# Experts in blocks of 32 rows on four column tiles, with smaller edits in the combination and the windowed attention

## The chip, the core and the metric

The kernel runs on one core of a Trainium2 chip. One launch computes everything. The metric is the time of one execution on the device, in microseconds (us). The engines named here are TensorE (PE; its weight loads are shown apart, as PEld), VectorE (DVE), ScalarE (ACT), GpSimd (POOL), and SyncE (SP), which issues most transfers.

## The reference, cut to what matters

The reference is a layer of two blocks on 1024 tokens of 1024 features, all in fp32. The first block mixes tokens by two gated scans and then runs a mixture of 32 experts; the second has a gated linear scan, a windowed attention, an RWKV scan and a feed-forward net. The change touches the mixture, the sum that follows it, and the windowed attention:

```
g_idx = argmax(g_logits)                      # one of 4 groups of 8 experts
top_v, top_i = top_k(e_in_group, 2)           # two experts of the group, for each token
weights = g_w * softmax(top_v)
gate, up = split(xb @ e_w_in[e], 2)           # 1024 -> 2 x 512
y = (silu(gate) * up) @ e_w_out[e]            # 512 -> 1024
out[token] += y * weight                      # two assignments of each token
...
o = sum over (window, dilation) in ((128,1),(512,4),(2048,16)) of softmax-weighted banded causal attention
```

There are 2048 assignments of a token to an expert. The routing formula, evaluated on the reference's own inputs, gives the experts between 2 and 447 tokens; the largest have 447, 282, 127, 122, 115, 94, 88 and 68. An expert's weights are 12 chunks of 128 rows and 1024 columns, 512 KB each: eight for the first product and four for the second.

## The kernel before, in words

The kernel is a chain of stages, each of which ends in a barrier of all engines. Within a stage every engine has its own list of instructions, and semaphores order them.

**Routing (`stage_route`).** It picks the experts, and places each assignment in a slot of a block. A block has `BR` = 64 slots and belongs to one expert; every expert has at least one block. DVE builds the tables `low` and `high` (L2098 to L2103), PE turns them into slot numbers (L1973), and DVE into row numbers for the gathers and scatters. The experts' order is computed here too: `seat` spreads those with many blocks among those with one, the two experts of number 0 and 1 come first.

**Experts (`stage_experts`).** Each of the blocks is computed as follows. POOL gathers its rows of the tokens from DRAM (L2227): partition p < 64 holds the first half of a row's features, partition 64 + p the second half, so that a gather has 128 descriptors of 2 KB. PE transposes the rows (`turn`, L2278), ACT copies them to `xt`. `up` (L2287) multiplies eight chunks of weights. The tokens are the stationary operand, only 64 columns wide, so PE's array is used as two column tiles: `lanes(j)` is the half of the columns, and of PSUM's partitions, on which the product with half j of the weights' columns runs. ACT applies silu and copies, POOL multiplies the two (L2236), PE transposes the result (`turn_h`, L2294), ACT copies it, and `down` (L2304) multiplies four chunks, again on two tiles. ACT copies the result to `y` (L2337), and POOL scatters it to the rows of `moe_y` (L2231).

The loop is pipelined in software. PE's order is `up(i+1)`, `turn(i+2)`, `down(i)`, `turn_h(i+1)`. POOL's order in iteration i is: multiply for block i+1; wait until every scatter issued so far has landed (`s_st`, L2250 and L2251), which frees `y`; wait for `turn(i+2)`, which frees `xr`; gather block i+3; wait for ACT's copy of block i; scatter block i. There is one buffer `xr` for gathered rows and one `y` for results.

The weights come by SP's queue. `raw` has two slots for each chunk, and `w`, from which PE reads, has one. DVE copies a chunk of the next expert from `raw` to `w` (L2210) as soon as the last block of the present one has used it. ACT copies the four chunks of the second product for every block anew (L2344). SP requests a chunk once DVE, or ACT at an expert's last block, has emptied its slot. So while an expert is computed the transfers can be two experts ahead and no further.

**Combination (`stage_combine`).** For each of the eight tiles of 128 tokens, SP loads the two results (three buffers of each), ACT weights the one (`weighted`, L2405), DVE adds the other (`summed`, L2447), PE transposes (L2500), and DVE adds into the residual (`added`, L2453). For each quarter of 256 tokens ACT squares (L2411), PE forms two sums of squares (`means`, L2509 and L2511), ACT takes roots, and DVE scales.

**Windowed attention (`stage_window`, after the gated scan).** SP requests queries and keys, the mask and the values in three transfers (L2851 to L2853). PE's first scores (L2869) wait for the whole of the first.

Of the kernel before, what the change touches and what calls it, by code (L numbers as in the profile page):

```python
# [42 lines left out]
BR = 64  # L43
# [1821 lines left out]
def stage_route(K):  # L1865
# [8 lines left out]
    with K.stage() as st:  # L1874
# [19 lines left out]
        far, wrap, yf, side = sb("far", [P, NS]), sb("wrap", [P, NS]), sb("slot", [P, NS]), sb("side", [P, 1])  # L1894
        pt = [K.ps(f"route_turn{i}", [P, 2, BANK], st) for i in range(2)]
# [16 lines left out]
        with nc.Block() as block:  # L1912
# [14 lines left out]
            def _(pool):  # L1927
                pool.memset(K.exp_rows[:], 0.0).then_inc(s_zero, 1)
                for s in s_st:
# [3 lines left out]
                pool.indirect_dma_start(K.exp_rows[:], None, xrows.rearrange("t (a d) -> (t a) d", a=2), bass.IndirectOffsetOnAxis(ap=K.moe_xi[:, 0:1], axis=0),  # L1933
                                        bounds_check=2 * T - 1, oob_is_err=False).then_inc(K.s_rows, 16)

            @block.tensor
            def _(pe):
# [32 lines left out]
                for u in range(NU):  # L1970
                    if u in (0, NU // 2):
                        pe.wait_ge(s_hot, 2 if u == 0 else 4)
                    mm = pe.matmul(pv, low[:, u, :], high[:, u, :], start=u == 0, stop=u == NU - 1)  # L1973
# [5 lines left out]
            def _(act):  # L1979
# [3 lines left out]
                for i in range(NT):  # L1983
# [4 lines left out]
                    if i == 0:  # L1988
                        act.wait_ge(s_step, 6)
# [5 lines left out]
            def _(dve):  # L1995
# [48 lines left out]
                step(dve.tensor_reduce(side[:], K.c("ident")[:, BR:P], AX.X, ALU.add))  # L2044
                dve.wait_ge(s_lt, 1)
# [71 lines left out]
                step(dve.tensor_scalar(far[:], wrap[:], 2.0, side[:], ALU.mult, ALU.add))  # L2117
                step(dve.tensor_copy(K.moe_xi[:], far[:]))
                dve.sem_inc(s_xi, 1)
                step(dve.tensor_scalar(yf[:], yf[:], 2.0, side[:], ALU.mult, ALU.add))  # L2120
# [23 lines left out]
def stage_experts(K):  # L2144
# [4 lines left out]
    HALF = D // 2  # L2149
    xrows = K.scratch["moe_x"].rearrange("t (a d) -> (t a) d", a=2)  # L2150
    yb = K.dram("moe_y", [2 * T, D]).rearrange("t (a d) -> (t a) d", a=2)
    KE, FH = DE // P, DE // 2
    UP, DOWN = range(KT), range(KT, NCHUNK)
    with K.stage() as st:
# [5 lines left out]
        xr, xt = K.exp_rows, sb("x", [P, KT // 2, P])  # L2160
        h, hu, ht, y = sb("h", [P, FH]), sb("h_up", [P, FH]), sb("h_turned", [P, KE // 2, P]), sb("y", [P, HALF])
        cx, cy = (K.sb(f"exp_{n}", [P, 1], I32, stack=st, fill=False) for n in ("x_at", "y_at"))
        pt, pu, ph, py = (K.ps(f"exp_{n}", [P, *shape], st) for n, shape in (
            ("turn", [KT // 2, P]), ("up", [2, FH]), ("turn_h", [KE // 2, P]), ("down", [BANK])))
# [12 lines left out]
        with nc.Block() as block:  # L2177
# [47 lines left out]
            def _(pool):  # L2225
                def gather(at):
                    pool.indirect_dma_start(xr[:], None, xrows, bass.IndirectOffsetOnAxis(ap=at, axis=0),  # L2227
                                            bounds_check=2 * T - 1, oob_is_err=False).then_inc(s_x, 16)

                def scatter(at):  # L2230
                    pool.indirect_dma_start(yb, bass.IndirectOffsetOnAxis(ap=at, axis=0), y[:], None,  # L2231
                                            bounds_check=4 * T - 1, oob_is_err=False).then_inc(s_st, 16)
# [2192 lines left out]
```

## Time and profile before

| | us |
|---|---|
| median of 3 runs (lowest to highest) | 3363.76 (3363.58 to 3369.75) |
| the profiled execution's own time | 3360.97 |
| its span, first to last instruction | 3359.2 |
| PE busy (share of the span) | 2964.2 (88%) |
| DVE busy | 1747.2 (52%) |
| ACT busy | 1263.9 (38%) |
| POOL busy | 302.4 (9%) |
| blocks of experts computed | 48 |

The span is divided into 40 slices of 84 us in the page. Busy shares are averages over stages with different limits, and PE's is high nearly everywhere. Each fp32 matmul of the program appears as two records, so a chunk of `up` on two tiles has four. A record's duration includes the time in which the last results leave the array, and records overlap: the pace is read from starts, not from durations.

### The profile page before, as it was taken

The page shows a single profiled execution, that of the slowest core. Times are in us where ns is not written, and L with a number is a line of the kernel's source. Part 1 is how long each engine was busy: PE and PEld are TensorE (multiplying, and loading weights), DVE is VectorE, ACT ScalarE, POOL GpSimd, SP SyncE. Part 2 cuts the span into 40 slices and gives each one's busy share as a digit, 9 for nine tenths or more (in the row PEclk, how much of TensorE's full clock was granted, in tenths as well). Part 3 has the DMA queues.
Part 4 walks back from the last instruction along what each step waited for, and adds up shares of the span by engine and source line. Part 5 has one row for each costly group of instructions (what it writes and reads, how often), then busy time and mean ns, then how long its engine had stood idle before and what let it go on. Part 6 is the DMA issues. An engine that isn't in the chain of part 4 may idle for free. (4 is left out here: it accounts for less than half of the span.)

```text
span 3359.2 us, 46984 instructions
## 1 busy us (share of the span) xinstructions
PE 2964.2 (88%) x17182; PEld 2107.5 (63%) x17183; DVE 1747.2 (52%) x2670; ACT 1263.9 (38%) x2003; POOL 302.4 (9%) x447
## 2 busy tenths in 40 slices
PE   7999789879699999967999598577979999799988
PEld 5788667756333333326888596266758888687766
DVE  6221664652543032427644684765468777634554
ACT  5220223341344545435433433411234454433423
POOL 2000002510022222310000000000000000000000
PEclk9999889889799999988999798789989999999999
DMA  6331663834599598962433211101122222153432
GB/s 216 102 108 57 181 208 132 219 96 168 208 399 408 229 409 346 384 266 73 128 104 91 69 48 51 66 3 59 57 75 90 80 87 83 62 217 134 170 102 86
DMA packets 342397, 509.82 MB, mean 152 GB/s; under 512 B 46525, under 2 KB 239492, under 8 KB 339024
## 3 DMA queue, kind: packets, MB, share of 16 engines
q1 hardware_dynamic: 308128, 436.81, 37.6%
q0 software_dynamic: 16336, 44.15, 3.5%
q10 hardware_dynamic: 17760, 26.48, 2.3%
q8 instruction: 117, 1.92, 0.2%
q14 instruction: 56, 0.46, 0.0%
HBM read 431.42 MB, written 85.10 MB: 154 GB/s over the span
## 5 line engine op out<-in xcount | busy, mean ns | idle before, releaser
L2287 PE MATMUL exp_up_psum<-exp_w,exp_x 128*64 128x512 f32 x1536 | 342.6, 599 | 5.1 <-issue 4.4
L2287 PEld LDWEIGHTS exp_up_psum<-exp_w,exp_x 128*64 128x64 f32 x1536 | 106.8, 137 | 207.3 <-issue 206.2
L2210 DVE COPY exp_w<-hN 128x1024 f32<-128x1024 f32 x128 | 89.1, 696 | 259.6 <-PE exp_up_psum L2287 237.8
L2344 ACT ACTIVATE exp_w<-exp_w_raw_down 128x1024 f32 x188 | 185.4, 1056 | 39.2 <-DMA exp_w_raw_down<-in_expert_w_out 39.0
L2304 PE MATMUL exp_down_psum<-exp_w,exp_h_turned 128*64 128x512 f32 x768 | 177.5, 600 | 8.2 <-ACT exp_w L2344 8.1
L421 PE MATMUL down_ps_psum<-down_ah,down_wh 128*128 128x512 f32 x352 | 141.3, 401 | 24.1 <-DVE down_al L4168 24.0
L2210 DVE COPY exp_w<-exp_w_raw_up 128x1024 f32<-128x1024 f32 x128 | 90.7, 713 | 122.4 <-PE exp_up_psum L2287 104.2
L421 PE MATMUL in_ps_psum<-hN_hi,in_wh 128*128 128x512 f32 x336 | 134.3, 400 | 5.6 <-DVE hN_lo L809 5.5
L422 PE MATMUL down_ps_psum<-down_al,down_wh 128*128 128x512 f32 x352 | 137.8, 391 | 0.0
L423 PE MATMUL down_ps_psum<-down_ah,down_wl 128*128 128x512 f32 x352 | 137.6, 391 | 0.0
L422 PE MATMUL in_ps_psum<-hN_lo,in_wh 128*128 128x512 f32 x336 | 132.1, 393 | 0.0
L423 PE MATMUL in_ps_psum<-hN_hi,in_wl 128*128 128x512 f32 x336 | 132.0, 393 | 0.0
L4166 DVE TENSOR_TENSOR down_wl<-down_w,down_wh 128x512 fp32r<-128x512 f32 (+1 forms) x66 | 57.4, 870 | 141.9 <-ACT down_wh L4137 141.8
L3998 DVE TENSOR_TENSOR up_wl<-up_w,up_wh 128x512 fp32r<-128x512 f32 x133 | 91.7, 690 | 74.9 <-ACT up_wh L3894 74.8
L421 PE MATMUL wout_ps_psum<-mixF_hi,wout_wh 128*128 128x512 f32 x256 | 105.6, 412 | 14.2 <-DVE mixF_lo L1784 12.9
L3650 DVE TENSOR_TENSOR in_wl<-in_w,in_wh 128x512 fp32r<-128x512 f32 x91 | 62.6, 690 | 105.0 <-ACT in_wh L3574 105.0
L2304 PEld LDWEIGHTS exp_down_psum<-exp_w,exp_h_turned 128*64 128x64 f32 x768 | 49.9, 136 | 101.8 <-issue 90.0
L3894 ACT ACTIVATE up_wh<-up_w 128x512 fp32r<-128x512 f32 x133 | 83.3, 627 | 72.4 <-PE up_z_psum L3860 32.6
L413 DVE CAST in_wh<-in_w 128x1024 fp32r<-128x1024 f32 x21 | 14.6, 693 | 182.5 <-PE in_ps_psum L423 182.5
L3860 PE MATMUL up_x_psum<-up_hi_T,up_wh 128*128 128x512 f32 x264 | 103.2, 391 | 2.0 <-DVE up_wl L3998 1.3
L4137 ACT ACTIVATE down_wh<-down_w 128x512 fp32r<-128x512 f32 (+1 forms) x66 | 51.0, 773 | 140.3 <-PE down_ps_psum L423 128.5
L3860 PE MATMUL up_x_psum<-up_hi_T,up_wl 128*128 128x512 f32 x264 | 102.7, 389 | 0.0
(829 smaller groups left out, 7438.7 us busy)
## 6 DMA issues: line engine op xcount, KB each, us to landing
exp_w_raw_up<-in_expert_w_in SPq DMA_DIRECT2D x128, 512.0 KB, 15.7
exp_w_raw_down<-in_expert_w_out SPq DMA_DIRECT2D x128, 512.0 KB, 15.5
hN<-in_expert_w_in SPq DMA_DIRECT2D x128, 512.0 KB, 15.5
in_w<-in_w_in SPq DMA_DIRECT2D x50, 512.0 KB, 4.0
up_w<-in_ffn_up SPq DMA_DIRECT2D x88, 256.0 KB, 3.4
down_a<-ffn_act SPq DMA_DIRECT2D x66, 256.0 KB, 3.3
down_w<-in_ffn_down SPq DMA_DIRECT2D x22, 512.0 KB, 3.4
down_w<-in_ffn_down SPq DMA_DIRECT2D x44, 256.0 KB, 2.6
```

The costliest lines, as they stand in the source:

```text
L421: pe.matmul(out, r(w[0]), r(x[0]), start=start, stop=False)
L422: pe.matmul(out, r(w[0]), r(x[1]), start=False, stop=False)
L423: return pe.matmul(out, r(w[1]), r(x[0]), start=False, stop=stop)
L2210: dve.tensor_copy(w[:, c, :], raw[u][c]).then_inc(s_have[c], 1)
L2287: mm = pe.matmul(pu[lanes(j), :, :], xt[:, c % (KT // 2), lanes(c // (KT // 2))], f[:, :, j * FH:(j + 1) * FH], start=c == 0, stop=c == KT ...
L2304: mm = pe.matmul(py[lanes(j), :], ht[:, k % (KE // 2), lanes(k // (KE // 2))], w[:, c, j * HALF:(j + 1) * HALF], start=k == 0, stop=k == K ...
L2344: act.activation(w[:, KT + k, :], K.exp_down[:, bass.ds(r + k, 1), :].rearrange("p o n -> p (o n)"), ACT.Copy).then_inc(s_down[k], 1)
L3650: dve.tensor_tensor(wl[i % R][:].bitcast(F32R), stationary[op](n), wh[i % R][:], ALU.subtract).then_inc(s_al, 1)
L3860: mm = pe.matmul(out, r32(w[r][:, k, :]), r32(v[o][:, k, :]), start=opens and k == 0 and x == 0, stop=k == 3 and x == 2, skip_group_check= ...
L3894: act.activation(wh[i % R][:].bitcast(F32R), stationary[op](n), ACT.Copy).then_inc(s_ah, 1)
L3998: dve.tensor_tensor(wl[i % R][:].bitcast(F32R), stationary[op](n), wh[i % R][:], ALU.subtract).then_inc(s_al, 1)
L4166: dve.tensor_tensor(wl[s % R][:, 0:n].bitcast(F32R), wt[s % R][:, 0:n], wh[s % R][:, 0:n], ALU.subtract).then_inc(s_wl, 1)
```

## The change

`BR` becomes 32 and the array is used as four column tiles of 32. A row of features is cut in four pieces of 256: a gather and a scatter still have 128 descriptors, now of 1 KB, and `up` and `down` have twice as many matmuls, each of half the columns. Products, copies and buffers of a block halve (`KX` = 2 transposes in `turn`, one in `turn_h`). The routing has room for 96 blocks in place of 64, so its tables are 98 wide in place of 66. POOL's and SP's loops, the number of buffers `xr`, `y`, `raw` and `w`, ACT's copies of the second product's weights for every block, and the formula of the experts' order stay as they are.

In the combination there are four buffers in place of three, and ACT's order changes. In the attention the three requests become seven, the first three of them small, and the waits are put where the pieces are used.

```diff
-BR = 64
+BR = 32
+NPART = P // BR
 NBLK = 2 * T // BR + NE
...
+                for a in range(2, NPART):
+                    step(dve.tensor_reduce(later[:], K.c("ident")[:, a * BR:P], AX.X, ALU.add))
+                    step(dve.tensor_tensor(side[:], side[:], later[:], ALU.add))
...
-                    for a in range(2):
+                    for a in range(NPART):
                         dve.tensor_tensor(low[:, u, a * BR:(a + 1) * BR], iota[:, 0:BR].unsqueeze(1).to_broadcast([P, NU // 2, BR]),
...
-    KE, FH = DE // P, DE // 2
+    KE, FH = DE // P, DE // NPART
+    KX, KH = KT // NPART, KE // NPART
...
-                    for k in range(KT // 2):
+                    for k in range(KX):
                         mm = pe.transpose(pt[:, k, :], xr[:, k * P:(k + 1) * P], K.c("ident"))
...
-                        for j in U:
-                            mm = pe.matmul(pu[lanes(j), :, :], xt[:, c % (KT // 2), lanes(c // (KT // 2))], f[:, :, j * FH:(j + 1) * FH],
+                        for j in range(NPART):
+                            mm = pe.matmul(pu[lanes(j), :, :], xt[:, c % KX, lanes(c // KX)], f[:, :, j * FH:(j + 1) * FH],
                                            start=c == 0, stop=c == KT - 1)
...
-                        for j in U:
-                            mm = pe.matmul(py[lanes(j), :], ht[:, k % (KE // 2), lanes(k // (KE // 2))], w[:, c, j * HALF:(j + 1) * HALF],
+                        for j in range(NPART):
+                            mm = pe.matmul(py[lanes(j), :], ht[:, k % KH, lanes(k // KH)], w[:, c, j * PIECE:(j + 1) * PIECE],
                                            start=k == 0, stop=k == KE - 1)
...
-    NT, NB, NQ = T // P, 3, 4
+    NT, NB, NQ = T // P, 4, 4
...
-                for i in range(3):
+                for i in range(NB):
                     weighted(i)
                 for q in range(NQ):
                     squares(q)
-                    for i in (2 * q + 3, 2 * q + 4):
+                    for i in (2 * q + 4, 2 * q + 5):
...
-                for i in range(3):
+                for i in range(NB):
                     turn(i)
                 for q in range(NQ):
-                    if 2 * q + 3 < NT:
-                        turn(2 * q + 3)
                     means(q)
-                    if 2 * q + 4 < NT:
-                        turn(2 * q + 4)
+                    for i in (2 * q + 4, 2 * q + 5):
+                        if i < NT:
+                            turn(i)
...
-                sp.dma_start(qkF[:], qk.rearrange("(a p) t -> p a t", p=P)).then_inc(s_qk, 16)
-                sp.dma_start(wide[:], K.wide_dram[:, 0:T]).then_inc(s_mask, 16)
-                sp.dma_start(v[:], vT[:, 512:768].rearrange("(c t) v -> t c v", t=P)).then_inc(s_v, 16)
+                sp.dma_start(qkF[:, 0::2, 0:EARLY], rows[0][:, :, 0:EARLY]).then_inc(s_qk[0], 16)
+                sp.dma_start(wide[:, T - EARLY:T], mask[:, T - EARLY:T]).then_inc(s_mask[0], 16)
+                sp.dma_start(v[:, 0:2, :], values[:, 0:2, :]).then_inc(s_v[0], 16)
+                sp.dma_start(qkF[:, 0::2, EARLY:T], rows[0][:, :, EARLY:T]).then_inc(s_qk[1], 16)
...
+                    if u in (0, 2, NT):
+                        pe.wait_ge(s_qk[(0, 2, NT).index(u)], 16)
```

PE in the body of the experts' loop, before (the text after a name is the shape of one matmul's output, xN their number; ISA is an instruction that only steers):

```order
L2287 MATMUL exp_up_psum<-exp_w,exp_x 64x512 x16
L2276 ISA
L2278 MATMUL exp_turn_psum<-const,exp_rows 128x128 x4
L2304 MATMUL exp_down_psum<-exp_w,exp_h_turned 64x512 x8
L2294 MATMUL exp_turn_h_psum<-const,exp_h 128x128 x2
```

And PE at the same place in the changed kernel:

```order
L2293 MATMUL exp_up_psum<-exp_w,exp_x 32x256 x32
L2282 ISA
L2284 MATMUL exp_turn_psum<-const,exp_rows 128x128 x2
L2310 MATMUL exp_down_psum<-exp_w,exp_h_turned 32x256 x16
L2300 MATMUL exp_turn_h_psum<-const,exp_h 128x128
```

Nothing changes places there: the matmuls are twice as many and cover a quarter of the output each, and the transposes are half as many.

In the combination PE's order stays, row by row. ACT's before, from its first tile to the squares of the second quarter (`comb_0` to `comb_2` are the three buffers; L2405 weights, L2411 squares):

```order
L2405 ACTIVATE comb_0<-comb_0,moe_w 128x1024
L2405 ACTIVATE comb_1<-comb_1,moe_w 128x1024
L2405 ACTIVATE comb_2<-comb_2,moe_w 128x1024
L2411 ACTIVATE comb_sq<-hF 128x2048
L2405 ACTIVATE comb_0<-comb_0,moe_w 128x1024
L2405 ACTIVATE comb_1<-comb_1,moe_w 128x1024
L2411 ACTIVATE comb_sq<-hF 128x2048
```

And ACT in the changed kernel:

```order
L2411 ACTIVATE comb_0<-comb_0,moe_w 128x1024
L2411 ACTIVATE comb_1<-comb_1,moe_w 128x1024
L2411 ACTIVATE comb_2<-comb_2,moe_w 128x1024
L2411 ACTIVATE comb_3<-comb_3,moe_w 128x1024
L2417 ACTIVATE comb_sq<-hF 128x2048
L2411 ACTIVATE comb_0<-comb_0,moe_w 128x1024
L2411 ACTIVATE comb_1<-comb_1,moe_w 128x1024
L2417 ACTIVATE comb_sq<-hF 128x2048
```

The fourth tile is now weighted ahead of the first squares, in a buffer of its own, and the others follow one place earlier too. Later on ACT the second quarter's roots come behind the squares of the last quarter, where they came before them.

SP at the attention's start, in the changed kernel:

```order
L2860 DMA win_qk<-bqk 128x2x256
L2861 DMA win_mask<-window_masks 128x256
L2862 DMA win_v<-viT 128x2x256
L2863 DMA win_qk<-bqk 128x2x768
L2864 DMA win_mask<-window_masks 128x768
L2865 DMA win_v<-viT 128x6x256
L2866 DMA win_qk<-bqk 128x2x1024
```

Before, there are three rows here, of 128x4x1024, 128x1024 and 128x8x256. PE's first scores wait for the first row in both kernels, and it is now an eighth as large.

## Rows read from the trace of the kernel before

**Rows 1.** Stretches: us, busy of each engine, PEclk, DMA share, GB/s.

```profile
903.00:1488.00 585.00, 561.47 (x2596) 187.15 (x2596) 179.75 (x256) 284.82 (x434) 164.25 (x242) 0.99 0.89 351
1000.00:1040.00 40.00, 40.00 (x190) 13.36 (x186) 16.85 (x24) 19.00 (x29) 12.13 (x16) 1.00 1.03 408
1120.00:1160.00 40.00, 40.00 (x190) 13.51 (x188) 0.00 (x0) 19.09 (x31) 11.62 (x19) 1.00 0.20 70
1488.00:1600.00 112.00, 72.35 (x310) 59.82 (x311) 78.40 (x159) 48.22 (x61) 0.00 (x0) 0.79 0.29 104
```

**Rows 2.** Timeline, PE, one block: start, us, instruction [idle before <-releaser].

```profile
929.08 0.44 PE L2294 MATMUL exp_turn_h_psum<-const,exp_h 128*128 128x128 f32 x2
929.45 7.09 PE L2287 MATMUL exp_up_psum<-exp_w,exp_x 128*64 128x512 f32 x32
...
937.05 3.65 PE L2304 MATMUL exp_down_psum<-exp_w,exp_h_turned 128*64 128x512 f32 x16
940.63 0.44 PE L2294 MATMUL exp_turn_h_psum<-const,exp_h 128*128 128x128 f32 x2
```

**Rows 3.** Tile exp_y over the whole span: ns min/median/max; the scatters' landing.

```profile
L2337 ACT ACTIVATE exp_y<-exp_down_psum x48: 597/597/616, 929.2 to 1482.7; 128x512 f32<-128x512 f32 x48
...
DMA to landing us min/median/max: 2.4/6.0/6.8
```

**Rows 4.** The scatters of 1120 to 1160 us alone.

```profile
DMA to landing us min/median/max: 2.8/2.8/2.8
```

**Rows 5.** Timeline, POOL: one block; a scatter, and the copy that waits for it.

```profile
1112.16 0.18 POOL L2253 COPY exp_x_at<-moe_x_rows 128x1 int32 x1
1113.19 1.08 POOL L2227 DMA_INDIRECT exp_rows<-moe_x,exp_x_at  x1 [0.85 <-POOL exp_x_at L2253]
1114.28 0.20 POOL L2257 COPY exp_y_at<-moe_y_rows 128x1 int32 x1
1115.39 1.03 POOL L2231 DMA_INDIRECT moe_y<-exp_y,exp_y_at  x1 [0.91 <-POOL exp_y_at L2257]
...
1478.30 1.03 POOL L2231 DMA_INDIRECT moe_y<-exp_y,exp_y_at  x1 [1.92 <-ACT exp_y L2337]
1481.26 0.18 POOL L2264 COPY exp_y_at<-moe_y_rows 128x1 int32 x1 [1.93 <-DMA moe_y<-exp_y,exp_y_at]
```

**Rows 6.** Timeline, PE: matmuls on four and on two column tiles elsewhere.

```profile
813.62 1.04 PE L214 MATMUL wout_mean_psum<-wout_gate_sq,cond_silu 128*1 128x512 f32 x8
...
2095.12 1.97 PE L2891 MATMUL win_out_psum<-win_probsT,win_v 128*64 128x128 f32 x32
```

**Rows 7.** The page's groups: ACT's copies of the second product's weights.

```profile
L2344 ACT ACTIVATE exp_w<-exp_w_raw_down 128x1024 f32 x188 | 185.4, 1056 | 39.2 <-DMA exp_w_raw_down<-in_expert_w_out 39.0
```

**Rows 8.** Waits of SP's queue, 903 to 1490: us in total, times, longest.

```profile
SPq L2141 <- DVE exp_w L2210: 107.2, 35, 50.5
```

**Rows 9.** The page's DMA issues: count, KB each, median us to landing.

```profile
exp_w_raw_up<-in_expert_w_in SPq DMA_DIRECT2D x128, 512.0 KB, 15.7
...
down_w<-in_ffn_down SPq DMA_DIRECT2D x44, 256.0 KB, 2.6
```

**Rows 10.** Timeline of the combination.

```profile
1511.47 1.91 ACT L2411 ACTIVATE comb_sq<-hF 128x2048 f32<-128x2048 f32 x1 [3.94 <-DVE hF L2453]
...
1514.52 1.28 DVE L2447 SCALAR_TENSOR_TENSOR comb<-comb,moe_w 128x1024 f32<-128x1024 f32 x1 [3.08 <-ACT comb L2405]
...
1517.62 5.61 PE L2509 MATMUL comb_means_psum<-comb_sq,const 128*128 128x256 f32 x16
```

**Rows 11.** Timeline of the attention's start.

```profile
2046.08 0.37 SPq L2851 DMA_DIRECT2D win_qk<-bqk  x1
...
2054.48 0.80 PE L2869 MATMUL win_s_psum<-win_qk 64*128 64x128 f32 x4 [13.39 <-DMA win_qk<-bqk]
```

**Rows 12.** Timeline of the routing: the tables, and PE's product of them.

```profile
884.86 1.26 DVE L2098 TENSOR_TENSOR route_high<-const,route_part 128x1056 f32<-128x1056 f32 x1
...
888.79 7.10 PE L1973 MATMUL route_mix_psum<-route_high,route_low 128*128 128x66 f32 x32 [6.86 <-DVE route_low L2103]
```

More of the change, by code:

```diff
@@ L2159, in stage_experts @@
         w = sb("w", [P, NCHUNK, 2 * DE])
-        xr, xt = K.exp_rows, sb("x", [P, KT // 2, P])
-        h, hu, ht, y = sb("h", [P, FH]), sb("h_up", [P, FH]), sb("h_turned", [P, KE // 2, P]), sb("y", [P, HALF])
+        xr, xt = K.exp_rows, sb("x", [P, KX, P])
+        h, hu, ht, y = sb("h", [P, FH]), sb("h_up", [P, FH]), sb("h_turned", [P, KH, P]), sb("y", [P, PIECE])
         cx, cy = (K.sb(f"exp_{n}", [P, 1], I32, stack=st, fill=False) for n in ("x_at", "y_at"))
         pt, pu, ph, py = (K.ps(f"exp_{n}", [P, *shape], st) for n, shape in (
-            ("turn", [KT // 2, P]), ("up", [2, FH]), ("turn_h", [KE // 2, P]), ("down", [BANK])))
+            ("turn", [KX, P]), ("up", [2, FH]), ("turn_h", [KH, P]), ("down", [PIECE])))
         s_raw = [[K.sem(f"exp_w_raw{u}_{c}") for c in range(NCHUNK)] for u in U]
@@ L2292, in turn_h @@
                     pe.wait_ge(s_h, b + 1)
-                    for k in range(KE // 2):
+                    for k in range(KH):
                         mm = pe.transpose(ph[:, k, :], h[:, k * P:(k + 1) * P], K.c("ident"))
@@ L2376, in stage_combine @@
         sq = [sb(f"sq{u}", [P, KT, QT]) for u in U]
-        ln1, rr = ([sb(f"{n}{u}", [P, QT]) for u in range(NQ)] for n in ("log", "root"))
+        ln1, rr = ([sb(f"{n}{u}", [P, QT]) for u in range(m)] for n, m in (("log", 2), ("root", NQ)))
         gsq, g12, gw, eps2 = sb("gain_sq", [P, KT]), sb("gains", [P, KT]), sb("gain_mean", [P, KT, P]), sb("eps_sq", [P, 1])
@@ L2537, in moe @@
         K.hN = K.sb("hN2", [P, KT, T], stack=weights)
-        K.exp_rows = K.sb("exp_rows", [P, D // 2], stack=weights)
+        K.exp_rows = K.sb("exp_rows", [P, D // NPART], stack=weights)
         K.s_rows = K.nc.alloc_semaphore("exp_rows_in")
@@ L2845, in stage_windows @@
         po = [K.ps(f"win_out{r}", [P, P], st) for r in U]
-        s_qk, s_mask, s_v, s_s, s_m, s_x, s_r, s_n, s_pt, s_pc, s_o, s_oc, s_st = (K.sem(f"win_{n}") for n in (
-            "qk", "mask", "v", "scores", "masked", "exp", "inv", "scaled", "turned", "copied", "o", "o_copied", "stored"))
+        EARLY = 2 * P
+        s_qk, s_mask, s_v = ([K.sem(f"win_{n}{u}") for u in range(m)] for n, m in (("qk", 3), ("mask", 2), ("v", 2)))
+        s_s, s_m, s_x, s_r, s_n, s_pt, s_pc, s_o, s_oc, s_st = (K.sem(f"win_{n}") for n in (
+            "scores", "masked", "exp", "inv", "scaled", "turned", "copied", "o", "o_copied", "stored"))
         with nc.Block() as block:
```

41 lines of the change are left out of this document (24 added, 17 removed).

## The prediction

> **What bounds the kernel now.** I read the stretches first, then PE's timeline inside the experts' stage, then the tile `exp_y`, POOL's timeline and the waits of SP's queue. The edits to the attention and the combination are worth a few us each; the experts' stage is 582 us long, from 904 to 1486, and decides. In it PE is busy for 561 of 585 us, but the transfers are near their limit as well: 351 GB/s on average, against 408 while they never pause [rows 1]. The reader should see both in one table: from 1000 to 1040 the DMA share is full, from 1120 to 1160 it is 0.20, and PE is fully busy in both. The quiet stretch lies in an expert of seven blocks, where SP's queue waits up to 50.5 us for DVE to empty a chunk [rows 8]: with two experts on hand nothing more can be asked for.
>
> One block takes PE 11.55 us, from 929.08 to 940.63 [rows 2]. There are 48 [rows 3], and 64-slot blocks counted from the routing of the reference's inputs are 48 too. 48 x 11.55 is 554; the other 28 us of the stage are its entry, its tail and the few places where PE waits for an expert's weights.
>
> **The experts, step by step.**
>
> *Number of blocks.* The same routing in blocks of 32 gives 78. The largest experts go from 7 and 5 blocks to 14 and 9.
>
> *PE's time for one.* `up` and `down` last 7.09 and 3.65; less 0.17 each, in which only the last results leave the array, that is 10.40 of the 11.55, or 0.87 for each of twelve chunks [rows 2]. A chunk will be streamed in half the columns on four tiles. That four tiles run side by side is in [rows 6]: the eight records of L214, 512 columns on four tiles, are over in 1.04 us, which is two steps of 0.43 and a way out of 0.17. That loads and matmuls can be issued fast enough is in the second row: 32 records in 1.97 us, less 0.17, are 0.056 us each, and a chunk of the new form needs eight in 0.43, 0.054 each. So a chunk costs 0.43, twelve cost 5.2, and the remaining 1.15 us (six transposes and the gaps) fall to about 0.8 with three. PE's block is 6.0 us. Bounds: 5.5 if the gaps shrink too, 6.9 if loop instructions that are hidden now show. By PE alone the stage would be 78 x 6.0 = 468, 86 us less than 554.
>
> *POOL's chain, which isn't changed.* A gather waits until the last scatter has landed. From the wait's end the rows give: 0.16 us to the next copy (at 1481.26, after a scatter of 1478.30 that takes the 2.8 of [rows 4]), then copy to gather 1.03, gather to copy 1.09, copy to scatter 1.11 [rows 5]. That is 3.39 from landing to the next scatter. Add the landing itself, L: a block can't be faster than L + 3.4. L is 6.0 us in the median [rows 3], and 2.8 in the stretch in which the weights' transfers rest [rows 4]. Before, 6.0 + 3.4 = 9.4 lies under 11.55 and is hidden by PE's work. After, it stands above 6.0 while weights stream. A scatter carries half the bytes but as many descriptors. I take 5.8, since the largest scatters are the slowest by some tenths; bounds 5.0 and 6.8 (the row's highest). So: 9.2 us a block while weights stream, 6.0 while they rest (PE's 6.0; the chain there has 2.8, or a little less for half the bytes, and 3.4).
>
> *How long weights stream.* 351 GB/s x 585 us = 205 MB; the change takes nothing from that. At 409 GB/s they need 502 us, whatever the blocks. In 502 us 502/9.2 = 54.6 blocks are done, and the other 23.4 take 6.0 each, 140 us. Together 642. The same sum for the kernel before gives 502/11.55 = 43.5 blocks and 4.5 x 11.55 more, 554, which is what it had apart from the 28. I carry the 28 over (bounds 12 and 28, as some of them are waits for weights that a slower chain hides): 670, or 88 us more than 582. With L = 5.0 it is 502 + 18.2 x 6.0 + 28 = 639, +57; with 6.8 it is 502 + 28.8 x 6.0 + 28 = 703, +121.
>
> *Other engines in that loop.* ACT's four copies for every block, 188 = 4 x 47 at about 0.97 us from start to start (1.056 long) [rows 7], stay 3.9 us; with its five shorter pieces at half size, about 1.1 us, it has 5.0 of the 6.0. It is hidden, but would be next. DVE's copies per expert are unchanged and wait for PE as before.
>
> *A rule against my sum.* The landing in the quiet stretch is 2.8 us and the median 6.0 [rows 3, 4]. The Trainium skill, "DMA: Bandwidth & Descriptors", section "Anatomy of one DMA — SWDGE (gpsimd) path", gives such a transfer about 2.0 us and its bytes at 436 GB/s, an estimate of 2.3 us for 128 KB here. The quiet rows agree within half a microsecond, the median doesn't. By the rule the chain would never show; that is rival 1.
>
> *The clock.* While PE works 6.0 of 9.2 us it is 65% busy. Between 1488 and 1600 it was 65% busy (72.35 of 112) and the granted clock was 0.79, so part of the time at 1.2 GHz; in the experts it was 0.99 [rows 1]. A block at 1.2 GHz needs 5.2 us more, 11.2, which is above 9.2; one with a third of it at that level fits. I book nothing, and keep it as rival 3.
>
> **The other edits.**
>
> *Routing.* DVE's table grows from 1056 to 1568 elements, 1.26 to about 1.87 us, twice: +1.2. PE's product has 98 columns in place of 66: 7.10 us becomes at most 10.5, and no more than before if the loads set it; halfway +1.7 [rows 12]. Sum +3. The steps for `side` lie ahead of the logits and are hidden.
>
> *Combination.* The first quarter's squares end at 1513.38, but its sums start at 1517.62, because PE stands at the fourth tile, which waits for DVE, which waits 3.08 us for ACT. With the tile weighted earlier the sums follow the squares: 4.2 us earlier [rows 10]. The rest of PE's chain is the same. -4; bounds 0 (DVE then sets the end) and -6.
>
> *Attention.* First scores at 2054.48, 8.4 us after the request at 2046.08 [rows 11]. 256 KB land in 2.6 us elsewhere [rows 9]; with the issue that is about 2049. The third unit needs the fourth request, 1.4 MB in all, 3.4 us at 409 GB/s, and it comes to it after some 4 us, so it doesn't wait. -5.5; bounds 0 and -6.
>
> **Sum.** 88 + 3 - 4 - 5.5 = +81.5. The profiled execution took 3361.0, which gives 3442.5; the median of the runs is 2.8 above it, so I say 3445.
>
> **Rivals.**
>
> 1. *The scatter's delay shrinks with the piece, so the chain is hidden.* For it: it does fall to 2.8 in quiet stretches. Against: the median is 6.0 with all sizes in it, and the streaming weights are the same. Then the limit is the transfers: 502 us streaming, plus what they must rest while two experts are on hand: 14 x 6.0 - 2 x 15.4 = 53 in the largest expert, 9 x 6.0 - 31 = 23 in the next (15.4 is 12 x 512 KB at 409), plus 12 for entry and tail: 590, +8. With the other edits +1.5: 3365. Even with the chain gone, the stage gains nothing.
>
> 2. *Faster.* As 1, and PE's block takes 5.4 us or less, so that the two long experts hold the transfers back less: 14 x 5.4 - 31 = 45 and 9 x 5.4 - 31 = 18, 502 + 63 + 12 = 577, -5; with the other edits -11.5: 3352. It needs a landing below 2.0 us (5.4 less 3.4) throughout, which no scatter of the trace had; it decides from about L = 2.
>
> 3. *The clock falls.* If the 54 blocks under streaming ran at 1.2 GHz, they would take 11.2 in place of 9.2: in 502 us 44.8 blocks, 33.2 left at 6.0: 199 in place of 140, +59: 3504. For it: the 0.79 above. Against: at 1.2 GHz PE has no gaps, and a PE without gaps was at 1.00 everywhere in this stage.
>
> 4. *The four tiles don't run side by side in this form*, and a block stays near 11.5: 78 x 11.55 + 28 = 929, +347: about 3700. [Rows 6] speak against it.
>
> **Chances.** Forecast (the chain shows, between the bounds of L) 0.76; rival 1 0.08; rival 2 0.05; rival 3 0.07; rival 4 0.04. The forecast's own range: +50 to +115 with the other edits, 3414 to 3478. To hold 8 in 10 I take a little of each neighbour: 3390 to 3488. What a measurement of this kernel can tell from no change is about 0.2%, 7 us. Faster 0.06, same 0.05 (most of rival 1 is within 7 us, part above), slower 0.89.
>
> **What would show it.** Starts of `turn` 9 us apart while the DMA share is full, with PE idle ahead of it for `exp_rows`, and 6 us apart while it is 0.2. A scatter landing in 5 to 6.5 us, POOL idle behind it. 78 copies to `exp_y`. Four chunks of `down` within 1.9 us. Sums in the combination within 1 us of the squares; first scores about 3 us after their request. It is wrong if landings under load are below 3 us, if PE has no gaps at `turn`, or if blocks come faster than 8.5 us beside streaming weights.

## The result, and the profile after

The kernel after takes 3454.16 us (median of 4 runs, 3449.14 to 3457.26) against 3363.67 for the kernel before on the same chip (3363.44 to 3369.75): a ratio of 1.0264, 95% interval 1.0251 to 1.0277, or +90.5 us. The forecast was 3445, +81.5.

Where the time of the profiled execution went, by first and last rows of each part (before, after, in us from the span's start):

| part | before | after | longer by |
|---|---|---|---|
| start of the experts' stage (first `turn`) | 903.94 | 904.68 | +0.7 |
| first `turn` to last scatter | 580.2 | 687.5 | +107.3 |
| last scatter to first matmul of the next projection | 79.6 | 70.4 | -9.2 |
| to the attention's first request | 482.3 | 482.5 | +0.1 |
| that request to the end of PE's last output matmul | 74.6 | 68.8 | -5.8 |
| the rest | | | +2.2 |

The parts add to +95.3, the difference of the two spans (3359.2 and 3454.5; the profiled executions took 3360.97 and 3456.33). So the experts' stage decides, as it did in the forecast. Its stretches after, to be read against [rows 1] (us, busy of each engine, PEclk, DMA share, GB/s):

```profile
903.00:1488.00 585.00, 460.04 (x6590) 232.94 (x6594) 145.51 (x216) 340.40 (x598) 215.66 (x331) 0.89 0.76 295
1000.00:1040.00 40.00, 29.71 (x426) 15.07 (x426) 19.33 (x29) 22.12 (x40) 15.75 (x21) 0.91 1.02 403
1160.00:1200.00 40.00, 38.96 (x634) 21.10 (x630) 0.00 (x0) 32.25 (x59) 18.13 (x31) 1.00 0.13 43
```

The second and third row are the pattern that was forecast. Where the weights stream (DMA share full), PE is busy for 29.7 of 40 us. Where they rest it is busy for 39.0. The first row has something for which I had booked nothing: the granted clock is 0.89, not 0.99.

PE's timeline after, one undisturbed block and then two under streaming (start, us, instruction, idle before it and its releaser), against [rows 2]:

```profile
930.92 3.66 PE L2293 MATMUL exp_up_psum<-exp_w,exp_x 128*32 128x256 f32 x64 [0.30 <-issue]
934.51 0.44 PE L2284 MATMUL exp_turn_psum<-const,exp_rows 128*128 128x128 f32 x2
934.88 1.93 PE L2310 MATMUL exp_down_psum<-exp_w,exp_h_turned 128*32 128x256 f32 x32
936.74 0.33 PE L2300 MATMUL exp_turn_h_psum<-const,exp_h 128*128 128x128 f32 x1
937.22 3.66 PE L2293 MATMUL exp_up_psum<-exp_w,exp_x 128*32 128x256 f32 x64
946.75 0.69 PE L2284 MATMUL exp_turn_psum<-const,exp_rows 128*128 128x128 f32 x2 [5.87 <-DMA exp_rows<-moe_x,exp_x_at]
947.37 3.64 PE L2310 MATMUL exp_down_psum<-exp_w,exp_h_turned 128*32 128x256 f32 x32
...
965.51 0.69 PE L2284 MATMUL exp_turn_psum<-const,exp_rows 128*128 128x128 f32 x2 [2.98 <-DMA exp_rows<-moe_x,exp_x_at]
966.13 3.13 PE L2310 MATMUL exp_down_psum<-exp_w,exp_h_turned 128*32 128x256 f32 x32
```

The block from 930.92 to 937.22 takes 6.3 us: four tiles do run side by side, and `down`'s four chunks take 1.93. At 946.75 PE has waited 5.87 us for a gather, and the same `down` then takes 3.64; the granted clock from 947.37 to 951.01 is 0.50, which is 1.2 GHz.

POOL's timeline, one pass after, against [rows 5]:

```profile
952.76 1.04 POOL L2237 DMA_INDIRECT moe_y<-exp_y,exp_y_at  x1 [0.91 <-POOL exp_y_at L2263]
956.04 0.44 POOL L2242 TENSOR_TENSOR exp_h<-exp_h,exp_h_up 128x128 f32<-128x128 f32 x1 [2.24 <-ACT exp_h_up L2334]
958.70 0.18 POOL L2259 COPY exp_x_at<-moe_x_rows 128x1 int32 x1 [2.21 <-DMA moe_y<-exp_y,exp_y_at]
959.73 1.07 POOL L2233 DMA_INDIRECT exp_rows<-moe_x,exp_x_at  x1 [0.85 <-POOL exp_x_at L2259]
...
961.91 1.02 POOL L2237 DMA_INDIRECT moe_y<-exp_y,exp_y_at  x1 [0.91 <-issue]
```

From scatter to scatter it is 9.15 us: 5.94 until the copy that waits for the landing starts, 3.21 from there to the next scatter. The tile `exp_y` gives the scatters' landing over all 78 blocks, against [rows 3], and the waits of the stage (us in total, times, longest) show who pays:

```profile
L2343 ACT ACTIVATE exp_y<-exp_down_psum x78: 383/383/385, 924.2 to 1590.9; 128x256 f32<-128x256 f32 x78
...
DMA to landing us min/median/max: 2.3/5.7/7.2
```

```profile
POOL exp_x_at L2259 <- DMA moe_y<-exp_y,exp_y_at: 166.8, 56, 5.5
...
PE exp_turn_psum L2284 <- DMA exp_rows<-moe_x,exp_x_at: 122.6, 45, 7.6
...
POOL moe_y L2237 <- ACT exp_y L2343: 5.5, 5, 1.4
```

The last of these is where a slow `down` of PE's holds up a scatter: POOL waits for ACT's copy of `down`'s result in five passes, 5.5 us in all.

I also took the 77 intervals between the starts of ACT's copies to `exp_y`. In the kernel after 54 of them are over 6.9 us, with a mean of 9.70, and 23 are below, with a mean of 6.22. I call these the 54 and the 23 from here on, and use the same positions for the experiments. The positions are sorted by this run's own times, so in any other run the long ones come out a little shorter and the short ones longer: e9, whose experts are the same, has 9.65 and 6.45. Sorted by the bytes moved, of POOL's 77 passes from scatter to scatter 48 run beside more than 300 GB/s, 6 beside 100 to 300, and 23 beside less than 100.

### The profile page after: what moved, and what is told of

Its sections match the earlier page's. It is cut to its first block and busy times, and to the rows that moved or that the text cites. A ratio compares the mean times of both kernels' runs of the same rounds, so it can differ in the third digit from the quotient of the medians.

```text
span 3454.5 us, 59055 instructions
## 1 busy us (share of the span) xinstructions
PE 2942.0 (85%) x22310; PEld 2191.8 (63%) x22311; DVE 1743.4 (50%) x2678; ACT 1381.0 (40%) x2273; POOL 395.1 (11%) x597
## 3 DMA queue, kind: packets, MB, share of 16 engines
q8 instruction: 118, 1.93, 0.2%
## 5 line engine op out<-in xcount | busy, mean ns | idle before, releaser
L2293 PE MATMUL exp_up_psum<-exp_w,exp_x 128*32 128x256 f32 x4992 | 297.0, 391 | 12.7 <-issue 11.4
L2350 ACT ACTIVATE exp_w<-exp_w_raw_down 128x1024 f32 x308 | 300.8, 1047 | 12.6 <-DMA exp_w_raw_down<-in_expert_w_out 12.5
L2293 PEld LDWEIGHTS exp_up_psum<-exp_w,exp_x 128*32 128x32 f32 x4992 | 159.4, 113 | 126.1 <-issue 32.4
L2310 PE MATMUL exp_down_psum<-exp_w,exp_h_turned 128*32 128x256 f32 x2496 | 192.8, 459 | 6.9 <-ACT exp_w L2350 6.9
L2284 PE MATMUL exp_turn_psum<-const,exp_rows 128*128 128x128 f32 x158 | 39.0, 333 | 132.7 <-DMA exp_rows<-moe_x,exp_x_at 122.6
L2310 PEld LDWEIGHTS exp_down_psum<-exp_w,exp_h_turned 128*32 128x32 f32 x2496 | 84.0, 127 | 86.1 <-issue 53.9
L2284 PEld LDWEIGHTS exp_turn_psum<-const,exp_rows 128*128 128x128 f32 x158 | 17.3, 154 | 168.2 <-DMA exp_rows<-moe_x,exp_x_at 146.5
```

Source lines behind the costliest of these rows:

```text
L2284: mm = pe.transpose(pt[:, k, :], xr[:, k * P:(k + 1) * P], K.c("ident"))
L2293: mm = pe.matmul(pu[lanes(j), :, :], xt[:, c % KX, lanes(c // KX)], f[:, :, j * FH:(j + 1) * FH], start=c == 0, stop=c == KT - 1)
L2310: mm = pe.matmul(py[lanes(j), :], ht[:, k % KH, lanes(k // KH)], w[:, c, j * PIECE:(j + 1) * PIECE], start=k == 0, stop=k == KE - 1)
L2350: act.activation(w[:, KT + k, :], K.exp_down[:, bass.ds(r + k, 1), :].rearrange("p o n -> p (o n)"), ACT.Copy).then_inc(s_down[k], 1)
```

## The experiments

The theory: POOL's chain (a scatter's landing, then the gather, then the next scatter) sets the pace while weights stream, and PE's gaps in it lower the clock, which may add some. The rivals: the clock alone; the transfers alone; POOL's own steps whatever the load.

### e1: the gather ahead of the wait

```diff
-                    pool.wait_ge(s_st, i * 16 + 16)
-                    pool.sem_inc(s_yfree, 1)
                     pool.wait_ge(s_t, i + 3)
...
                     gather(cx[:])
+                    pool.wait_ge(s_st, i * 16 + 16)
+                    pool.sem_inc(s_yfree, 1)
                     pool.tensor_copy(cy[:], K.moe_yi[:, bass.ds(i, 1)]).then_inc(s_at, 1)
```

> The kernel after, with one move: in POOL's loop the gather goes out before the wait for the last scatter's landing, not behind it. Theory (the chain landing -> gather -> next scatter sets the pace while weights stream): the chain splits in two that run side by side. The scatter's own: landing 5.8 + about 1.3 (copy of the row numbers, 0.91 of waiting, issue) = 7.1 us. The gather's own: about 5.8 from issue to the transposes, 0.5 for them, 1.1 to the next gather = 7.4 us. So a block under streaming falls from about 9.4 to 7.4; 502 us hold 67 blocks, 11 are left at 6.3: 571 + 28 = 599 us for the stage in place of 688, total about 3365 to 3375. Rival A (the lower granted clock, 0.82 to 0.92 in the streaming stretches, sets PE's pace): PE's own work is what takes the time, less than 15 us are won, total 3440 or more. Rival B (weights' transfers set it): nothing is won, 3454.

3415.46 us, ratio to before 1.0149 (1.0128 to 1.0170): 39 us less than the kernel after. More than the clock or the transfers alone allowed, but half of what the theory said. Its waits, 903 to 1590:

```profile
PE exp_turn_psum L2284 <- DMA exp_rows<-moe_x,exp_x_at: 74.2, 45, 3.1
...
ACT exp_w L2350 <- DMA exp_w_raw_down<-in_expert_w_out: 42.1, 32, 8.9
```

PE still waits for gathers in as many blocks, 1.6 us each in place of 2.7, and ACT has begun to wait for weights. The 54 take 8.71 us, not 7.4. From the first `turn` to the last scatter it is 645.5 us, against 687.5; e5 below, which has no chain left, gets no lower than 630.7, so most of what is missing to the theory's 599 isn't POOL's.

### e2: two buffers for y

```diff
-        h, hu, ht, y = sb("h", [P, FH]), sb("h_up", [P, FH]), sb("h_turned", [P, KH, P]), sb("y", [P, PIECE])
-        cx, cy = (K.sb(f"exp_{n}", [P, 1], I32, stack=st, fill=False) for n in ("x_at", "y_at"))
...
+        h, hu, ht, y = sb("h", [P, FH]), sb("h_up", [P, FH]), sb("h_turned", [P, KH, P]), [sb(f"y{u}", [P, PIECE]) for u in U]
+        cx, cy = ([K.sb(f"exp_{n}{u}", [P, 1], I32, stack=st, fill=False) for u in U] for n in ("x_at", "y_at"))
...
-                    pool.wait_ge(s_st, i * 16 + 16)
+                    pool.wait_ge(s_st[u], m)
```

`s_st` has a semaphore for each buffer, and `m` is the count of the scatter before last.

> The kernel after, with two buffers for exp_y and for its row numbers, used in turn (the loops of POOL and ACT take two blocks a pass; the number of blocks is taken as even, and is 78): POOL waits for the scatter before last, so that no scatter's landing stands in the chain; the gather still has one buffer. Theory: the gather's loop of 7.4 us is left, as in the first kernel; stage about 600, total 3365 to 3375, within 10 us of the first. If the scatter's landing alone was the matter and gathers are quick, blocks fall to 6.3 and the stage to the transfers' 590. Rival A (clock): 3440 or more. Rival B (transfers): 3454.

3412.64 us, 1.0144 (1.0123 to 1.0165): the same as e1, as said; the size is missed in the same way. Once a scatter doesn't hold up the next gather, taking its landing out of the chain altogether gives nothing more. PE's wait for gathers is 67.9 us.

### e3: the two small edits without the experts

The combination and the attention as in the kernel after, everything else as before.

> The kernel before, with the edits to the combination and to the attention alone; the experts stay in blocks of 64. From the two traces: combination -9 (from the last scatter to the first matmul of the projection 79.6 us before, 70.4 after), attention -4: 3351. Rival: part of the 9 us belongs to the smaller last scatters of the blocks of 32 (3 of them lie ahead of the first transposes), then the combination gives 6 and the total is 3354 or more. As forecast before the result: -4 and -5.5, also 3354.

3355.24 us, 0.9970 (0.9959 to 0.9981), 8.5 us less than before. The rival's value holds. PE's timeline of e3, against [rows 10]; the sums start at 1513.34 in place of 1517.62:

```profile
1511.58 1.97 PE L2500 MATMUL comb_ps_psum<-const,comb 128*128 128x128 f32 x8 [1.29 <-DVE comb L2447]
1513.34 5.64 PE L2509 MATMUL comb_means_psum<-comb_sq,const 128*128 128x256 f32 x16
```

From the first transposes to the projection it is 60.1 us before and 55.8 here. In the attention the first scores come 2.7 us after the first request in place of 8.4, and the last output 3.8 us earlier against that request. The third unit now stands 2.2 us for the fourth request:

```profile
2043.34 0.80 PE L2878 MATMUL win_s_psum<-win_qk 64*128 64x128 f32 x4 [7.72 <-DMA win_qk<-bqk]
...
2048.43 1.65 PE L2878 MATMUL win_s_psum<-win_qk 64*128 64x384 f32 x4 [2.23 <-DMA win_qk<-bqk]
```

### e4: half the weights

```diff
-                        request_expert(K, sp, raw[u][c], c, e, s_raw[u][c])
+                        if c % 2:
+                            sp.sem_inc(s_raw[u][c], 16)
+                        else:
+                            request_expert(K, sp, raw[u][c], c, e, s_raw[u][c])
```

The same stands in the loops for both products' chunks.

> The kernel after, with every second chunk of the experts' weights not loaded from the third expert on (its semaphore is raised in place of the transfer; the copies and products stay, so the products use stale weights: only time is read from it). Halves the bytes under which gathers and scatters travel. Theory (landing beside saturated transfers makes the chain long): landings fall towards the 2.5 us of the quiet stretches, the chain to about 6, under PE's 6.3; 78 x 6.3 + 28 = 519, total about 3285; granted clock about 1.0. Rival A (the chain is long from POOL's own steps, not from the weights' transfers): blocks of 9.2 stay, stage about 680, total 3450. Rival C (the clock falls by itself in this form of matmul): clock stays 0.89 and blocks stay above 7 us, total above 3330.

3388.57 us (one run). The landing's median is 4.4 in place of 5.7, the clock in the stage 0.91, the 54 take 8.32. The time misses the theory's 3285 by 100 us, though nothing but the weights' load was changed, and rival A's 3450 fails too. Rival C's numbers fit (blocks above 7 us, total above 3330), so this run alone doesn't remove it; e6 and e10 do. The stretch 1000 to 1100 shows why the theory fell short: the transfers left still come in bursts (DMA share 0.75 there).

```profile
1000.00:1100.00 100.00, 79.04 (x1148) 40.11 (x1152) 37.71 (x57) 58.11 (x104) 41.29 (x60) 0.90 0.75 262
```

### e5: two buffers for the gathered rows too

The centre of its edit against e2:

```diff
-        xr, xt = [K.exp_rows], sb("x", [P, KX, P])
+        xr, xt = [K.exp_rows, sb("rows1", [P, PIECE])], sb("x", [P, KX, P])
...
-                    pool.tensor_copy(cx[0][:], K.moe_xi[:, bass.ds(i + 3, 1)]).then_inc(s_at, 1)
+                    pool.tensor_copy(cx[u][:], K.moe_xi[:, bass.ds(i + 4, 1)]).then_inc(s_at, 1)
```

> The kernel of e2_two_y with two buffers for exp_rows as well (and for its row numbers), so that a gather is asked for two blocks ahead. Theory: in e2 the gather's own loop was what was left (PE waits 68 us for exp_rows in 42 blocks). With it gone PE has no wait for DMAs of POOL's, works closely enough that the granted clock returns to 0.97 or more, and the stage is held by the weights' transfers alone: 590 to 605 us from 904 to the last scatter (646 in e2), total 3360 to 3375. Rival A (the clock is low in this form of matmul whatever the gaps): clock stays about 0.92 and the stage above 625, total 3390 or more. Rival B (gathers queue behind scatters in POOL's DMA queue, so a second buffer helps little): waits for exp_rows stay above 40 us, 3395 or more.

3396.95 us, 1.0091 (1.0074 to 1.0108). The waits for gathers are gone except the first (6.0 us), so rival B is out. The stage still isn't at 600: last scatter at 1536.38. What PE waits for now (903 to 1540), and the stretch 1000 to 1100:

```profile
PE exp_down_psum L2319 <- ACT exp_w L2363: 53.7, 50, 6.4
```

```profile
1000.00:1100.00 100.00, 78.25 (x915) 31.88 (x909) 30.59 (x46) 51.75 (x85) 30.00 (x46) 0.76 1.03 408
```

ACT in turn waits 101.9 us for the weights, the transfers are full, and the clock beside PE's new gaps is 0.76. The bound is now the weights, as the theory had it, but at 632 us (from 904) and not at 590 to 605. Rival A's numbers (stage above 625, total 3390 or more) fit this run as well; e6 and e10 have the same matmuls at a clock of 0.99, and remove it.

### e6: no weights

As e4, with no chunk requested from the third expert on.

> The kernel after, with no load of experts' weights from the third expert on (semaphores raised in its place; copies and products stay and use stale weights: only time is read from it). Theory: every landing is as in the quiet stretches, 2.3 to 3; POOL's chain is 2.5 + 3.4 = 5.9, under PE's block of 6.3; all 77 intervals lie between 6.0 and 6.9, 78 x 6.3 + 20 = 511 us from 904 to the last scatter, total about 3280; clock about 1.0. Rival A (chain long by itself): median interval 7.5 or more. Rival C (clock falls by itself): clock below 0.95, `down` in the mean above 2.2 us.

3275.12 us (one run), the last scatter at 1415.68, 511 us after the first `turn` at about 905. POOL's timeline in it, a whole pass and the landing of the next scatter:

```profile
999.36 1.16 POOL L2237 DMA_INDIRECT moe_y<-exp_y,exp_y_at  x1 [0.91 <-POOL exp_y_at L2263]
1001.62 0.92 POOL L2242 TENSOR_TENSOR exp_h<-exp_h,exp_h_up 128x128 f32<-128x128 f32 x1 [1.09 <-ACT exp_h_up L2334]
1002.49 0.64 POOL L2259 COPY exp_x_at<-moe_x_rows 128x1 int32 x1
...
1006.50 1.16 POOL L2237 DMA_INDIRECT moe_y<-exp_y,exp_y_at  x1 [0.91 <-POOL exp_y_at L2263]
1008.50 0.58 POOL L2242 TENSOR_TENSOR exp_h<-exp_h,exp_h_up 128x128 f32<-128x128 f32 x1 [0.84 <-ACT exp_h_up L2334]
1009.41 0.25 POOL L2259 COPY exp_x_at<-moe_x_rows 128x1 int32 x1 [0.34 <-DMA moe_y<-exp_y,exp_y_at]
```

The copy that waits for the landing starts 2.9 us after the scatter at 1006.50, where it was 5.94 in the pass shown above, and POOL hardly waits for it. The Trainium skill's rule that the forecast weighed ("DMA: Bandwidth & Descriptors", section "Anatomy of one DMA — SWDGE (gpsimd) path", an estimate of 2.3 us from its figures) agrees within 0.6 us with this run's 2.9 and with the quiet stretches (2.8 in [rows 4], there for 256 KB), and not with the median of 5.7 beside streaming weights. PE's `down` and the stretch:

```profile
L2310 PE MATMUL exp_down_psum<-exp_w,exp_h_turned 128*32 128x256 f32 x2496 | 151.5, 382 | 2.4 <-ACT exp_w L2350 2.4
```

```profile
1000.00:1100.00 100.00, 95.50 (x1540) 51.50 (x1536) 30.43 (x45) 77.88 (x142) 51.04 (x79) 1.00 0.11 35
```

`down` is 1.94 us a block, the clock 1.00 here and 0.99 from 903 to 1400. Rivals A and C are both out: neither POOL's steps nor this form of matmul are slow by themselves. Twelve intervals are between 6.9 and 7.8, so "all below 6.9" was too strict.

### e7: the gaps filled

```diff
-                def turn(b):
+                def turn(b, more=0):
+                    for k in range(more):
+                        pe.transpose(pt[:, k % KX, :], K.c("ident"), K.c("ident"))
                     pe.wait_ge(s_x, b * 16 + 16)
...
-                    turn(i + 2)
+                    turn(i + 2, 8)
```

> The kernel after, with eight more transposes of the identity (about 1.8 us of PE) in each block, ahead of PE's wait for the gather: the chain of POOL isn't touched. Theory (chain plus a clock that falls in PE's gaps): in blocks under streaming the added work lies in the gap, the clock rises from 0.89 to 0.95 or more, `down` goes from 2.46 us a block in the mean (192.8 / 78) to below 2.1; those intervals fall from 9.7 to about 9.2 although PE has more to do, while the 23 quiet ones rise from 6.2 to 8.0. Net about 54 x -0.5 + 23 x 1.8 = +15, total 3455 to 3475. Rival A (`down` is slow from contention with the transfers, not from the clock): `down` stays at 2.4, intervals under streaming stay at 9.7 or grow, total 3490 or more.

3465.93 us (one run), in the range. The four runs of e9 are 10 us apart, so a single total 12 us above the kernel after's says little; the trace says more. PE's lines of `down` in the kernel after and in this one (busy us, mean ns, idle before):

```profile
L2310 PE MATMUL exp_down_psum<-exp_w,exp_h_turned 128*32 128x256 f32 x2496 | 192.8, 459 | 6.9 <-ACT exp_w L2350 6.9
```

```profile
L2312 PE MATMUL exp_down_psum<-exp_w,exp_h_turned 128*32 128x256 f32 x2492 | 173.0, 423 | 3.2 <-ACT exp_w L2352 3.2
...
L2283 PE MATMUL exp_turn_psum<-const 128*128 128x128 f32 x616 | 84.1, 279 | 0.0
```

With 84 us more work PE has 20 us less in `down`, at a clock of 0.94 in place of 0.89 (903 to 1590). So `down` was slow because of the clock, not because of the transfers, and the clock is a consequence of the gaps: rival A is out. `down` fell to 2.22, not below 2.1, since the added work is 1.1 us a block and not the 1.8 that I had written down.

What the low clock costs the kernel is another question. The 54 fall from 9.70 to 9.48 and the 23 rise from 6.22 to 7.23; 54 x -0.22 + 23 x 1.01 = +11, which is what was measured. But part of this is only the sorting of the positions (above), and POOL's passes didn't get shorter: beside more than 100 GB/s there are 53 with a mean of 9.71 us, in the kernel after 54 with a mean of 9.59. POOL even waits longer for landings than the 166.8 us of the kernel after:

```profile
POOL exp_x_at L2259 <- DMA moe_y<-exp_y,exp_y_at: 188.5, 57, 5.7
```

So the added work cost nothing where it lay in a gap, and the higher clock won nothing that POOL's passes show. That the low clock costs the kernel something by itself isn't shown.

### e8: blocks of 64 with the gather first

The edit of e1 in the kernel of e3.

> The kernel of e3_small_edits (blocks of 64), with the gather ahead of the wait for the scatter, as in e1. Theory (POOL's chain, 9.4, is hidden under PE's block of 11.55): nothing changes, 3355 within 3 us; e1's gain of 40 us belongs to the small blocks alone. Rival (the chain also holds up blocks of 64 here and there, where PE idles 23 us in the stage before): up to 10 us are won, 3345.

3353.02 us, 0.9967 (0.9954 to 0.9981): 2 us below e3, with intervals that cover each other, so a small gain isn't told apart from none; the 39 us of e1 aren't there. With blocks of 64 POOL's chain costs next to nothing, as the forecast had it (9.4 under 11.55). This and e3 are the versions that beat both kernels.

### e9: the experts' change alone

The kernel after with the combination and the attention of before.

> The kernel after without its two small edits: combination and attention as before, experts (and routing) in blocks of 32. If the parts add up, this is the kernel after plus what e3 won (8.5): 3462 to 3464, +99 against before. Rival: part of the combination's shorter stretch after (54 us in place of 60) comes from the scatters of the small blocks or from the clock, and not from its edit; then the parts don't add up and it is below 3461.

3465.98 us, 1.0315 (1.0297 to 1.0333): +102. Against it the kernel after is 12 us faster, e3 is 8.5 faster than before: the parts add up within 3.5 us. It is 2 us above the range given, on the side away from the rival (below 3461), which fails. From the first transposes to the projection it is 58.8 us here and 54.1 after.

### e10: both buffers doubled and half the weights

> e5 and e4 together: two buffers for exp_rows and exp_y, and every second chunk of weights not loaded from the third expert on (stale weights in those: only time is read from it). It closes the square of chain and weights: 3454 with both in full, 3388 with half the weights, 3397 with the chain out of the way. Theory (in e5 only the weights' transfers are left): blocks at 6.1 to 6.6 nearly throughout, stage 510 to 535 us, total 3280 to 3300, clock in the stage 0.97 or more. Rival A (something else is left in e5, such as PE's own work at the low clock or ACT's copies): stage above 560, total 3325 or more.

3275.76 us (one run), a little under the theory's 3280 to 3300; the 54 take 6.37. The stretch 903 to 1400:

```profile
903.00:1400.00 497.00, 474.58 (x7592) 254.65 (x7592) 173.42 (x256) 385.34 (x688) 258.00 (x385) 0.99 0.62 223
```

The square of causes is closed by the place of the last scatter:

| last scatter at, us | all weights | half the weights |
|---|---|---|
| one buffer each (chain) | 1592.2 (after) | 1528.0 (e4) |
| two buffers each (no chain) | 1536.4 (e5) | 1412.9 (e10) |

Removing the chain gives 56 us with all weights and 115 with half; halving the weights gives 64 with the chain and 124 without. Either one alone leaves the other as the bound, which explains the shortfall of e4 and the greater part of e1's and e2's. With both gone, 78 x 6.3 + 20 = 511 is reached (1412.9 - 904 = 509).

## Why the prediction was right, and where it wasn't

**PE's block.** 6.0 forecast; 6.1 and 6.5 in turn in quiet stretches, mean 6.22. Four tiles side by side, and a chunk at about half the time: right. The 0.3 us at every second `up`, for which nothing is recorded, was inside the upper bound ("loop instructions that are hidden now show").

**POOL's chain.** The mechanism is the forecast's. L = 5.8 forecast, 5.7 measured, both in the median of all 78 and in that of the 48 passes beside more than 300 GB/s. From the copy that follows the landing to the next scatter it is 3.23 by the forecast's rows and 3.21 in the pass shown; 9.2 a block forecast, 9.15 in that pass. That the same landing is long only beside streaming weights is shown by e4 and e6; that the chain binds, by e1, e2 and e5; that it was hidden before, by e8.

**The count.** 54.6 blocks under streaming and 23.4 at PE's pace were forecast; 54 and 23 were found, by the intervals and by the bytes alike.

**The stage, +88 forecast, +107 measured.** By its own terms: the 54 took 523.6 us in place of 502, the 23 took 143.1 in place of 140, and entry and tail 20.8 in place of 28. Together 687.5 in place of 670. The mis-sized term is the 9.2 us of a pass under streaming, which the forecast took for all of them from a median landing and from POOL's steps in one block. The 48 passes beside more than 300 GB/s have a median of 9.38 and a mean of 9.67 us: 48 x 0.47 = +23. On average the copy starts 6.28 us after the scatter (5.96 forecast, with 0.16 from landing to copy), and the next scatter 3.39 after it (3.23 forecast). Three things can be read in POOL's timeline. One pass, 1073.21 to 1089.57, takes 16.36 us, because PE waits for ACT's copies of the weights and ACT 8.21 us for their transfer: +7. In five of the first passes after a rest of the transfers the copy starts only 6.6 to 7.5 us after the scatter. And in 13 passes POOL's own steps take 3.5 to 4.3 us; where DVE copies weights at the same time, a gather is issued in 1.43 us (1105.80) in place of 1.08. Whether DVE's copies are the cause wasn't tested.

**The clock.** The forecast booked nothing for it, and its argument was wrong: a gap and a slow block don't exclude each other, since the gap comes first and the instruction behind it (`down` at 947.37) is slow. `down` took 192.8 us against 151.5 in e6, `up` 297.0 against 286.9, the two transposes 66.7 against 60.5: 58 us of PE's time in all. But nearly all of it lies in time that PE would have waited anyway: in 45 of the 48 passes the last thing that POOL's copy waits for is the landing, and POOL's scatters wait 5.5 us in all for `down`'s result. So booking nothing came out nearly right, but not for the reason given. Rival 3 saw the clock fall, and its price (+59) took all streaming blocks at 1.2 GHz.

**Rival 1's floor.** It said that with the chain gone the stage would be 590 and the kernel 3365. e5 took the chain away and stood at 632 and 3397. This is the worst number of the forecast, though it hung on no chance. The floor was 502 + 53 + 23 + 12, and e5's trace says which terms were short:

```profile
920.00:940.00 20.00, 19.69 (x293) 10.11 (x285) 5.55 (x8) 11.24 (x23) 7.76 (x13) 0.91 0.29 96
1127.00:1202.00 75.00, 73.22 (x1178) 39.15 (x1172) 5.38 (x8) 58.13 (x106) 34.56 (x58) 0.99 0.26 91
1364.00:1402.00 38.00, 36.82 (x599) 19.77 (x595) 5.13 (x8) 30.13 (x54) 18.10 (x30) 1.00 0.27 97
1518.00:1536.00 18.00, 14.70 (x230) 7.20 (x229) 5.37 (x8) 14.30 (x24) 8.76 (x14) 1.00 0.20 76
```

Against 408 GB/s the transfers miss 58 and 29 us in the two largest experts (53 and 23 forecast; blocks of 6.3 in place of 6.0 give 57 and 26). At the entry they miss 15 in the first of these rows and 6 from 904 to 920, and 15 at the tail: 36 in place of 12. So the entry and the tail are most of the error, and not other experts. These rows show no part of the clock in it: it is 0.99 and 1.00 in the two long rests, and the 0.76 lies where the transfers are full.

**The small edits.** Combination -4 forecast; -4.3 (e3) and -4.7 (after against e9). The rest of the 9.2 belongs to the experts' change: the first transposes come 16.3 us after the last scatter in place of 19.5, in e9 16.0; and the first sums last 4.23 us after and 5.61 before. Attention -5.5 forecast; -3.8 in e3, -5.9 after against e9. "The third unit doesn't wait" was wrong: it waits 2.2 us for the fourth request, as seen in e3, which takes a part of what the first scores win.

**Routing.** +3 forecast, +0.7 found. DVE's two steps for `high` grew by 0.53 us each (0.61 forecast), but `low` fell from 2.50 to 1.77, which the forecast left out, and PE's product didn't grow:

```profile
884.83 1.79 DVE L2103 TENSOR_TENSOR route_high<-const,route_part 128x1568 f32<-128x1568 f32 x1
```

```profile
889.97 7.12 PE L1975 MATMUL route_mix_psum<-route_high,route_low 128*128 128x98 f32 x32 [8.07 <-DVE route_low L2108]
```

7.12 us with 98 columns and 7.10 with 66 [rows 12]: the lower of my two bounds, I had taken the middle.

The forecast's sum of +81.5 stands against +95.3 between the profiled executions: +19.3 in the stage, -5.2 on the way to the projection, -2.3 in the routing, -0.3 in the attention, and +2.3 elsewhere. Between the medians it is +90.5, 9 us above the forecast. That it comes so near is partly luck: the stage's +19 is offset by terms that have nothing to do with it.

## What to carry to other kernels

Before making a pipeline's step shorter, list every loop that runs beside it and isn't made shorter (here landing, gather, scatter: 9.2 us a pass against a step that went from 11.55 to 6.3), and read that loop's latency where the memory is loaded, not in the quiet stretches. Where two things each take nearly the whole stage, one experiment that removes one of them will seem to disprove it; take both away as well. A slow instruction behind a gap of TensorE's need not cost the kernel anything: before giving the lower clock a price, look at who waits for that instruction (here a scatter, 5.5 us in all, while PE's own time grew by 58).

## What was unexpected of the hardware

- The landing of a 128 KB scatter of POOL's depends on the load by the weights' transfers of SP's: median 5.7 us with all of them, 4.4 with half. With none only the time from the scatter to the copy that waits for it can be read, 2.9 us where it was 5.94.
- A wait of 5.87 us for a gather was followed by a `down` of 3.64 us in place of 1.93. Over the stage the granted clock was 0.89 with a wait for a gather at 45 of 78 blocks, 1.00 in the quiet stretches and in e6 (1000 to 1100), and 0.76 where PE waited for weights inside a block (e5, 1000 to 1100).
- A matmul of 98 columns took as long as one of 66 where every one has weights of its own (32 records in 7.12 and 7.10 us).
